# GpSimd takes over the mixing of FFN blocks and one sum of kept products, in an encoder step on one Trainium2 core

## The reference, cut to what matters

```
def swiglu(x, g, w_gu, w_down):
    gu = rmsnorm(x, g) @ w_gu                       # w_gu: 1024 x 5632
    return (jax.nn.silu(gu[..., :D_FF]) * gu[..., D_FF:]) @ w_down   # w_down: 2816 x 1024
...
x = x + jnp.concatenate([op, om], axis=-1) @ w_out[i]
x = x + swiglu(x, g_ffn[i], w_gu[i], w_down[i])
```

## Time and profile before

| what | value |
|---|---|
| median of 3 runs | 1237.77 us (1237.73 to 1237.99) |
| the profiled execution's own time | 1238.03 us |
| its span, first to last instruction | 1236.2 us |
| granted TensorE clock, mean | 0.997 of full speed |
| TensorE busy | 1214.3 us, 98% |
| VectorE busy | 987.5 us, 80% |
| ScalarE busy | 655.2 us, 53% |
| GpSimd busy | 83.5 us, 7% |
| steady pairs of the first layer | 279.4 to 539.4 us of the span |
| steady pairs of the second layer | 937.8 to 1197.8 us |

### The profile page before, as it was taken

How to read it: one execution, slowest core, us unless ns; L and a number is a source line. 1 busy time by engine, 2 the same in 40 slices (tenths; PEclk the granted TensorE clock), 3 DMA queues, 4 the chain that set the end, 5 groups by cost and what they waited for, 6 DMA issues and landing times.

```text
span 1236.2 us, 23212 instructions
## 1 busy us (share of the span) xinstructions
PE 1214.3 (98%) x9050; PEld 1171.3 (95%) x9050; DVE 987.5 (80%) x1601; ACT 655.2 (53%) x1180; POOL 83.5 (7%) x117
## 2 busy tenths in 40 slices
PE   7999999999999999999999999999999999999997
PEld 7998999999999999999989986899999999999997
DVE  6767557999999999975775477557999999999962
ACT  5657434455555555555764467534554555555542
POOL 2000000002001001102001100000001000100103
PEclk9999999999999999999999999999999999999999
DMA  7243122216325433525344210122225433532622
GB/s 225 70 137 122 52 86 86 69 54 151 108 77 119 118 94 93 141 80 164 120 137 127 86 55 2 34 78 81 67 62 134 117 94 92 127 103 82 155 68 85
DMA packets 197132, 122.14 MB, mean 99 GB/s; under 512 B 6307, under 2 KB 189251, under 8 KB 197024
## 3 DMA queue, kind: packets, MB, share of 16 engines
q1 hardware_dynamic: 185792, 101.23, 27.8%
q0 software_dynamic: 11040, 19.37, 7.0%
q10 hardware_dynamic: 192, 0.06, 0.0%
HBM read 106.67 MB, written 6.90 MB: 92 GB/s over the span
## 4 chain that ended last, share of the span: by engine, by line
PE 88%; DVE 6%; issue 2%; ACT 2%; DMA 0%; ACTq 0%; DVEq 0%
PE ACCP L1833 31%; PE ACCP L1854 22%; PE MISC L1854 21%; PE ACCP L1949 3%; PE ACCP L2102 3%; PE ACCP L2073 2%; PE MISC L1870 2%; PE MISC L2044 1%; PE MISC L2057 1%; DVE EL L1456 1%; DVE WL L1425 1%; PE MISC L1876 1%; DVE BL L1754 1%; PE MISC L2061 1%; ACT EH L1107 1%
## 5 line engine op out<-in xcount | busy, mean ns | idle before, releaser
L1089 ACT ACTIVATE WH<-RAW 128x1024 fp32r<-128x1024 f32 (+2 forms) x149 | 144.2, 968 | 126.7 <-PE ACCP L1833 108.9
L1107 ACT ACTIVATE EH<-SB 128x1024 fp32r<-128x1024 f32 (+1 forms) x116 | 112.7, 971 | 157.4 <-DVE SB L1450 70.1
L1425 DVE TENSOR_TENSOR WL<-RAW,WH 128x1024 fp32r<-128x1024 f32 (+2 forms) x148 | 165.8, 1120 | 19.0 <-ACT WH L1089 18.0
L1456 DVE TENSOR_TENSOR EL<-SB,EH 128x1024 fp32r<-128x1024 f32 (+1 forms) x116 | 128.7, 1110 | 5.4 <-ACT EH L1107 3.4
L1833 PE MATMUL ACCP<-XH,WH 128*128 128x288 f32 x512 | 111.2, 299 | 0.9 <-DVE XL L1568 0.9
L1833 PE MATMUL ACCP<-XH,WL 128*128 128x288 f32 x512 | 109.7, 296 | 0.0
L1833 PE MATMUL ACCP<-XL,WH 128*128 128x288 f32 x512 | 109.6, 296 | 0.0
L1854 PE MATMUL MISC<-BH,EH 128*128 128x288 f32 x360 | 106.8, 297 | 1.6 <-DVE EL L1456 1.5
L1854 PE MATMUL ACCP<-BH,EH 128*128 128x288 f32 x360 | 106.5, 296 | 0.0
L1854 PE MATMUL MISC<-BL,EH 128*128 128x288 f32 x360 | 106.2, 295 | 0.0
L1854 PE MATMUL ACCP<-BL,EH 128*128 128x288 f32 x360 | 106.2, 295 | 0.0
(11 more groups left out here) (350 smaller groups left out, 3474.0 us busy)
## 6 DMA issues: line engine op xcount, KB each, us to landing
RAW<-in_w_gu SPq DMA_DIRECT2D x88, 512.0 KB, 4.1
RAW<-in_w_down SPq DMA_DIRECT2D x48, 384.0 KB, 3.8
RAW<-in_w_in SPq DMA_DIRECT2D x16, 512.0 KB, 4.0
RAW<-in_w_mem_kv SPq DMA_DIRECT2D x16, 512.0 KB, 3.7
RAW<-in_w_out SPq DMA_DIRECT2D x16, 512.0 KB, 3.9
X<-PC POOLq DMA_DIRECT2D x48, 144.0 KB, 3.1
RAW<-in_w_down SPq DMA_DIRECT2D x16, 256.0 KB, 2.9
RAW<-in_w_kv SPq DMA_DIRECT2D x8, 512.0 KB, 3.7
```

Of the source, the lines that this page charges most:

```text
L1089: a.activation(panel_in(WH, w % SPLIT_SLOTS, p), panel_in(RAW, p % RAW_SLOTS, p), ACT.Copy).then_inc(split_ready(w, True)[0], 1)
L1107: a.activation(EH[:, first:first + n, 0:nh], mixtures(s)[:, first:first + n, 0:nh], ACT.Copy).then_inc(block_hi, n)
L1425: v.tensor_tensor(panel_in(WL, w % SPLIT_SLOTS, p), panel_in(RAW, p % RAW_SLOTS, p), panel_in(WH, w % SPLIT_SLOTS, p), ALU.subtract).then_ ...
L1456: v.tensor_tensor(EL[:, first:first + n, 0:nh], mixtures(s)[:, first:first + n, 0:nh], EH[:, first:first + n, 0:nh], ALU.subtract).then_in ...
```

## The change

`mix_blocks(k)` and one of the sums of a gu pair go from VectorE's queue to GpSimd's.

- GpSimd, in a gu pair with a k, does the four mixing operations; in every gu pair, after them, it waits for the three kept products and adds product 1 to product 2 in `PC`, and counts `kept_summed`. For the leads it mixes at `prepare_blocks`. (A down pair would mix too if it had a k.)
- VectorE loses `mix_blocks` and `third_sum`. `second_sum` now also waits for `kept_summed`, and adds the sum of both kept products at once.
- `copies_used` of a gu pair, which says when `PC` may be overwritten, goes by `u_ready` (second_sum) instead of `up_right` (third_sum).

```
@@ GpSimd
+            def mix_blocks(k):
+
+                t = HBT[k % HPAIRS]
+                twos = HPAIRS * MIXED_PARTS
+                gp.wait_ge(h_ready, k // twos * FC + 2 * (k % twos) + 2)
+                g.tensor_tensor(t[:, 2], t[:, 5], t[:, 1], ALU.subtract).then_inc(hidden_mixed, 1)
+                gp.wait_ge(hidden_mixed, 4 * k + 1)
+                g.tensor_tensor(t[:, 1], t[:, 1], t[:, 0], ALU.subtract).then_inc(hidden_mixed, 1)
+                gp.wait_ge(hidden_mixed, 4 * k + 2)
+                g.tensor_tensor(t[:, 3], t[:, 5], t[:, 1], ALU.subtract).then_inc(hidden_mixed, 1)
+                gp.wait_ge(hidden_mixed, 4 * k + 3)
+                g.tensor_tensor(t[:, 6], t[:, 4], t[:, 3], ALU.subtract).then_inc(hidden_mixed, 1)
...
+                elif s.kind == "pair" and s.which == "gu":
+                    if s.k is not None:
+                        mix_blocks(s.k)
+                    gp.wait_ge(copied, 3 * s.i + 3)
+                    g.tensor_tensor(PC[:, s.i % 2, 2], PC[:, s.i % 2, 2], PC[:, s.i % 2, 1], ALU.add).then_inc(kept_summed, 1)
+                elif s.kind == "prepare_blocks":
+                    mix_blocks(s.k)
                 elif s.kind == "pair" and s.which == "down":
+                    if s.k is not None:
+                        mix_blocks(s.k)
@@ VectorE
-            def mix_blocks(k):
...
                 dve.wait_ge(copied, 3 * s.i + 3)
                 dve.wait_ge(u_ready, 2 * s.i + 1)
+                dve.wait_ge(kept_summed, s.c + 1)
                 v.tensor_tensor(TU[:, HALF:T], U1[:], PC[:, s.i % 2, 2], ALU.add).then_inc(u_ready, 1)
-
-            def third_sum(s):
-
-                dve.wait_ge(u_ready, 2 * s.i + 2)
-                v.tensor_tensor(TU[:, HALF:T], TU[:, HALF:T], PC[:, s.i % 2, 1], ALU.add).then_inc(up_right, 1)
...
-                elif s.kind == "prepare_blocks":
-                    mix_blocks(s.k)
...
-                        if s.k is not None:
-                            mix_blocks(s.k)
...
-                        third_sum(s)
@@ shared
-            return (up_right, s.c + 1) if s.which == "gu" else (x22_done, 16 * (s.c + 1))
+            return (u_ready, 2 * s.i + 2) if s.which == "gu" else (x22_done, 16 * (s.c + 1))
```

More of the change, by code:

```diff
@@ L748, in encoder_kernel @@
         block_done, copied = sem("block_done"), sem("copied")
-        u_ready, up_right, crossed = sem("u_ready"), sem("up_right"), sem("crossed")
+        u_ready, kept_summed, crossed = sem("u_ready"), sem("kept_summed"), sem("crossed")
         gate_right = sem("gate_right")
```

## The result

The kernel after takes **1269.91 us** (1267.93 to 1270.2), the kernel before on the same chip 1237.75 (1237.71 to 1237.99): a ratio of 1.0257 (95% interval 1.0245 to 1.027), slower. The forecast was 1281 with a range of 1242 to 1302. The profiled execution has a span of 1268.4 us against 1236.2 before: 32.2 us more.

A forecast was written before the change was run, and what follows sets the result against it. TensorE was taken to bound the kernel, VectorE just behind. Four series (32.8 us) and the layers' starts (9.8) summed to 42.6 us, added to the profiled 1238.03 less 0.26: about 1281 us, range 1242 to 1302.

The forecast's parts named there:

- What bounds the kernel, and the gain at most: Steady pairs: TensorE sets the time, a lighter VectorE gains nothing; some 4 us at most, at the layers' starts.
- The slack: Mixing pairs: 1.2 us for the next pair's first `EL`, 0.6 for its second, 0.8 for `HBL` before down pairs.
- Exclusion: VectorE and GpSimd operations with two SBUF inputs exclude each other whole; at 0.69 us, mixtures some 5.5 us after `hidden`.
- The series: Three mixing pairs, two series a layer: stalls 2.0, 3.0, 2.9 us, 8.2 with small ones; 32.8 in all.
- The start of a layer: Two mixing pairs in a row: stalls 2.2 and 4.8, 7.0 instead of 2.1 us; +4.9 a layer, 9.8 in all.
- The clock: TensorE's clock stays at its upper level, since the trace's stalls of 1 us left it there; no cost.
- the signs named: Profile after: `HBH` 5 to 6 us after `hidden`, TensorE waits of 2 to 3 us, plain pairs without stall.
- The kept sum: Plain pairs: GpSimd's one add costs VectorE 0.69 us by exclusion, less 0.49 saved; no stall there.
- GpSimd's DMAs, SP's loads and the prepared mixings of the leads: DMAs for down pairs, loads waiting for `EL`, and the two lead mixings: nothing lost on any of them.
- Side by side: Rival, chance 0.15: engines do not hinder each other, mixtures 3.3 us after `hidden`; 1236 to 1241 us.
- Heavier: Rival, chance 0.10: fixed price per GpSimd operation, such as 0.5 us for starting; +32 us, about 1313.
- Half way: Rival, chance 0.12: GpSimd waits only for the operation in flight, VectorE never; stalls 0.3 to 1.4 us, 1242 to 1262.

The follow-up runs named there:

- experiment 5: Changed kernel with GpSimd's four mixing operations replaced by memsets of the same 288 columns (FFN mixtures not computed): 1233.1 us, one execution.
- experiment 1: Changed kernel with the third sum back on VectorE, so that only the mixing is on GpSimd: 1275.24 us, ratio 1.0306 to the kernel before.
- Experiment 4: Changed kernel with GpSimd's mixing of k 1 in each layer made to wait for gu 5's `hidden`: 1278.33 us, ratio 1.0327 to the kernel before.
- experiment 2: Kernel before with only the kept sum moved to GpSimd, all mixing staying on VectorE: 1238.82 us, ratio 1.0008.
- experiment 7: Kernel before with GpSimd mixing only k 1 of each layer, in gu 4, all else on VectorE: 1236.0 us, ratio 0.9988.
- experiment 3: Changed kernel with VectorE waiting, in mixing pairs, for GpSimd's fourth mixture before its panel operations: 1261.63 us, ratio 1.0193 to the kernel before.

## Why the prediction was right, and where its sum was not

**What bounds the kernel, and the gain at most:** right. The steady stretches gained nothing from a lighter VectorE, and the ceiling measured 4.5 us (experiment 5, one execution).

**The slack** (1.2, 0.6 and 0.8 us): right. The stalls are for the first `EL` and for `HBL`, in the places named; `HBL` starts 2.6 us late, and less the 1.2 that leaves 1.4, where TensorE waits 1.35; the 0.6 of the second `EL` shows in experiment 1.

**Exclusion:** right in kind, too long in size. I took a GpSimd operation to hold VectorE off for the whole of its length, at 0.69 us. The length is 0.80, above my value and inside the bounds (0.43 to 0.89), but it holds VectorE for 0.61 only. With turns of 1.22 instead of 1.38 the mixtures came 4.9 after `hidden`, not 5.5. The rule cited from the Trainium skill (SBUF — State Buffer, "Who interferes with whom") agrees with the 1.30 against 0.68 here, and also with the memset's 0.68 in experiment 5. The estimate scaled from the Trainium skill (GPSIMD Engine Reference, section 3.1; 0.63) agrees with the 0.61 held and not with the length of an instruction alone, 0.80.

**The series** of three mixing pairs: 8.2 us each was the term; they measured 5.3, 6.5, 5.3 and 5.6. The first stall was 1.5 to 1.9 for 2.0, the second 2.3 to 2.7 for 3.0, the third 1.5 to 2.3 for 2.9. Sum 22.7 for 32.8: **-10.1**. The cause is the 0.6 us of each mixing and, for the third, the clock's falls, during which VectorE catches up. The forecast's own steps, redone with 4.9 for 5.5 and 0.61 for the plain pair's 0.69, give stalls of 1.4, 2.3 and 2.2 us, 6.2 a series with the small ones; the series without a fall measured 6.5, the three with one 5.3 to 5.6.

**The start of a layer:** wrong step. "First: hidden ends ..., `HBL` starts 257.8" took GpSimd's mixing to wait for gu 5's `hidden`, because VectorE's did. It has its own queue and the data was a pair old. No stall in gu 6's second block, then 3.1 for the 4.8; against 2.0 lost there before, +1.1 a layer for the forecast's +4.9: **-7.6** in all. Experiment 4 shows it: with GpSimd made to wait for gu 5's `hidden`, 1.56 and 1.46 us are lost there, and 4.0 at the first down block.

**The clock:** wrong. "The clock stays at its upper level: the trace's stalls of 1 us left it there" reasoned from stalls of 1 us to stalls of 2 to 3. Four falls: **+5.9**. What is left, 1.1, I put down to small distances over 134 ns.

Together 42.6 - 10.1 - 7.6 + 5.9 + 1.1 = 31.9, the measured lateness. The result was in the range, with errors that partly cancelled: without the falls, and without the 0.8 us that each of three gave back at a third stall, it would have been 31.9 - 5.9 + 2.4 = 28.4. Two of the signs named were missed narrowly: `HBH` starts 4.95 us after `hidden`, not 5 to 6, and the first stall of a series is 1.5 to 1.9, not 2 to 3.

**The kept sum** was as forecast in plain pairs (experiment 2), and helped by 5 us where VectorE was late (experiment 1). GpSimd's DMAs, SP's loads and the prepared mixings of the leads cost nothing, as forecast: in the pairs TensorE has no wait for any of them.

**The rivals.** Side by side was excluded by the 1.30 us. Heavier was not borne out: between dependent operations GpSimd leaves 0.08 us. Half way (4 to 4.7 us after `hidden`) was nearer than its 0.12 says: the measured 4.9 lies between it and the forecast.

## What to carry to other kernels

A step goes to another engine for nothing only if its result is due later than the slower engine gives it: measure the slack of that step's consumer (here 1.2 us), not the busy share of the engine that is relieved (94%). Price an operation on GpSimd beside VectorE at the length that it adds to VectorE's too, and look at what VectorE runs at that moment: two SBUF inputs on both sides are the costly pair, and a mixing that costs 2 us of stall in one pair is free where it is due a pair later. And when an instruction changes its engine, ask anew which data and which queue it waits for; it may run much earlier than at its old place.

## What the runs showed of the hardware that was not expected

- **GpSimd holds VectorE up for less than its instruction's length.** An add of 288 columns takes 0.80 us alone and adds 0.61 to 0.62 to VectorE's operation beside it (0.68 to 1.30).
- **Who goes first isn't even.** In gu 8 GpSimd gets in after one VectorE operation. In gu 4 its first (240.59, above) takes 3.31 us, to 243.90, and VectorE's unbroken run of operations ends at 243.23, 0.67 before; experiment 7's first there takes 2.38, and ends 0.67 after such a run too. In gu 8 the first GpSimd operation ends at 323.12, 0.67 after VectorE's first. What decides between turns and waiting for the whole run wasn't settled.
- **TensorE's clock falls after some stalls of 2 to 4 us.** After the change it fell four times after a stall of 2.3 to 3.1 us, for 3.4 us at half speed; but three stalls of the same size had no such effect. With the traces of experiments 1 and 4, 14 of 22 stalls of 2.1 to 4.0 us were followed or met by a fall, for 3.4 or 6.8 us. A stall of 2.68 us was followed by one in the kernel after, and one of 2.68 in experiment 4 was not, so what tells them apart stays open. No stall under 2 us was, and in experiment 3, whose longest is 1.6 us, the clock did not fall in the pairs.
